# The mLSTM norm of a hybrid decoder layer in one piece of four chunks, with the last numerators between the two halves of the last output-gate product

## The reference, cut to what matters

```
h   = num / max(|den|, exp(-m))
mu  = mean(h);  var = mean((h - mu)^2)            # per token and head, 128 values
h   = (h - mu) * rsqrt(var + LN_EPS) * ml_norm_g
y_ml = sigmoid(o_m) * h                            # o_m: output-gate projection of the stream
q_lat = einsum('bthd,hdc->bthc', q_a, w_uk)        # queries of the attention, per head
s = einsum('bqhc,bqkc->bqhk', q_lat, kv_sel) * scale; p = softmax(s)
return concat([y_att, y_ml]) @ w_out
```

## Time and profile before

| what | value |
|---|---|
| median of 3 runs | 1124.44 us (1123.28 to 1125.76) |
| profiled execution, its own time | 1123.59 us |
| its span, first to last instruction | 1121.9 us |
| mean granted TensorE clock | 0.985 |
| TensorE busy | 1079.1 us (96%) |
| VectorE busy | 468.6 us (42%) |
| ScalarE busy | 347.4 us (31%) |
| GpSimd busy | 134.1 us (12%) |

### The profile page before, as it was taken

How to read it: one execution, slowest core, us unless ns; L and a number is a source line. 1 busy time by engine, 2 the same in 40 slices (tenths; PEclk the granted TensorE clock), 3 DMA queues, 4 the chain that set the end, 5 groups by cost and what they waited for, 6 DMA issues and landing times.

```text
span 1121.9 us, 15986 instructions
## 1 busy us (share of the span) xinstructions
PE 1079.1 (96%) x6569; PEld 931.7 (83%) x6569; DVE 468.6 (42%) x725; ACT 347.4 (31%) x453; POOL 134.1 (12%) x98
## 2 busy tenths in 40 slices
PE   8999999999999999999988999999999999999993
PEld 7999999999999987689865568768888888888882
DVE  3332332323232253699885533553333333322235
ACT  3222322222121234434337532452223232221211
POOL 4000000000011115212313004240000000000001
PEclk9999999999999999989998999999999999999997
DMA  6424233231322323122210101223333333143311
GB/s 191 113 75 111 76 87 100 75 100 52 104 79 86 106 75 97 38 79 73 76 38 1 38 1 46 67 75 89 99 92 95 96 91 100 59 134 89 92 51 75
DMA packets 159165, 90.34 MB, mean 81 GB/s; under 512 B 6596, under 2 KB 156792, under 8 KB 159128
## 3 DMA queue, kind: packets, MB, share of 16 engines
q1 hardware_dynamic: 159128, 89.83, 28.1%
HBM read 87.72 MB, written 2.10 MB: 80 GB/s over the span
## 4 chain that ended last, share of the span: by engine, by line
PE 88%; DVE 6%; ACT 3%; POOL 2%; issue 1%; DMA 0%; DVEq 0%; SPq 0%; POOLq 0%
PE ps L919 75%; PE ps L1054 4%; POOL xl L484 2%; PE ps L1328 2%; PE ps L1308 1%; PE ps L1319 1%; DVE x L1545 1%; DVE zrow L1503 1%; PE ps L1336 1%; DVE sil L1539 1%; PE ps L1116 1%; ACT whi L617 1%; DMA xin<-in_x 0%; DVE x L1528 0%; PE ps L1218 0%
## 5 line engine op out<-in xcount | busy, mean ns | idle before, releaser
L919 PE MATMUL ps<-xl,whi 128*128 128x264 f32 (+1 forms) x1264 | 350.9, 330 | 8.9 <-POOL xl L484 8.0
L919 PE MATMUL ps<-xh,whi 128*128 128x264 f32 (+1 forms) x1264 | 356.1, 331 | 2.7 <-DVE wlo L1412 1.6
L919 PE MATMUL ps<-xh,wlo 128*128 128x264 f32 (+1 forms) x1264 | 353.3, 329 | 0.0
L919 PEld LDWEIGHTS ps<-xl,whi 128*128 128x128 f32 x1264 | 212.4, 190 | 36.4 <-POOL xl L484 16.1
L919 PEld LDWEIGHTS ps<-xh,whi 128*128 128x128 f32 x1264 | 212.8, 189 | 30.0 <-issue 5.9
L919 PEld LDWEIGHTS ps<-xh,wlo 128*128 128x128 f32 x1264 | 213.8, 189 | 21.7 <-issue 0.2
L1403 DVE TENSOR_TENSOR wlo<-wraw,whi 128x2048 fp32r<-128x2048 f32 (+1 forms) x81 | 171.5, 2117 | 144.0 <-ACT whi L617 144.0
L617 ACT ACTIVATE whi<-wraw 128x2048 fp32r<-128x2048 f32 (+1 forms) x89 | 152.4, 1712 | 129.6 <-PE ps L919 123.8
L919 PE MATMUL ps<-hh,whi 128*128 128x264 f32 (+1 forms) x528 | 141.5, 322 | 0.0
L919 PE MATMUL ps<-hl,whi 128*128 128x264 f32 (+1 forms) x528 | 141.2, 321 | 0.0
L919 PE MATMUL ps<-hh,wlo 128*128 128x264 f32 (+1 forms) x528 | 140.4, 320 | 0.0
(11 more groups left out here) (217 smaller groups left out, 873.8 us busy)
## 6 DMA issues: line engine op xcount, KB each, us to landing
wraw<-in_ffn_w_gate SPq DMA_DIRECT2D x44, 512.0 KB, 4.0
wraw<-in_ffn_w_up SPq DMA_DIRECT2D x43, 512.0 KB, 5.2
wraw<-in_ffn_w_down SPq DMA_DIRECT2D x32, 384.0 KB, 3.4
wraw<-in_ffn_w_down SPq DMA_DIRECT2D x32, 320.0 KB, 3.8
wraw<-in_w_in SPq DMA_DIRECT2D x19, 512.0 KB, 4.7
wraw<-in_w_out SPq DMA_DIRECT2D x8, 512.0 KB, 4.0
xin<-in_x SPq DMA_DIRECT2D x2, 1024.0 KB, 6.1
out<-zrow SPq DMA_DIRECT2D x8, 256.0 KB, 2.0
```

The lines of the kernel that those rows point to most:

```text
L919: mm = pe.matmul(ps[:, b + e, 0:width], w, mov, start=(first and n == 0), stop=(last and n == 2))
```

## The change

The numerators of chunk 4 move from behind the whole product `o_half(19)` to between its fourth and fifth step. On ScalarE their copy `copy_num(4)` moves ahead of the sigmoid `o_out(19)`, and the square root, which was taken once before that sigmoid (three chunks) and once between the copies of the latent queries (the last chunk), is taken once behind the sigmoid, for all chunks. On VectorE the norm is one piece of four chunks; the operations that apply it are moved into the attention: heads 0 and 1 (eight operations) ahead of group 0, heads 2 and 3 (eight operations) behind the first two masked scores.

```
 # ScalarE
                 copy_num(3)
-                mlstm_sd(0, 3)
+                copy_num(4)
                 o_out(19)
-                copy_num(4)
+                mlstm_sd()
                 for h in range(ATT_H):
-                    if h == 4:
-                        mlstm_sd(3, 4)
                     act.wait_ge(ql_done, h + 1)
...
-            def mlstm_sd(j0, j1):
-                act.wait_ge(ml_var, 1 if j0 == 0 else 2)
-                v = mls[:, 0, :].rearrange("p (h j) -> p h j", h=ML_H)[:, :, j0:j1]
-                act.activation(v, v, ACT.Sqrt).then_inc(ml_sd, 1)
+            def mlstm_sd():
+                act.wait_ge(ml_var, 1)
+                act.activation(mls[:, 0, :], mls[:, 0, :], ACT.Sqrt).then_inc(ml_sd, 1)
 # TensorE
                 numerators(3)
-                o_half(19)
+                o_half(19, 0, 4)
                 numerators(4)
+                o_half(19, 4, KT)
                 lat_queries()
 # VectorE
-                mlstm_norm(0, 3)
-                normed_mlstm(range(ML_H), 0, 3)
-                mlstm_norm(3, 4)
+                mlstm_norm()
...
+            def mlstm_norm():
+                for j in range(4):
                     dve.wait_ge(num_copied, 2 * (j + 1))
                     for h in range(ML_H):
                         dve.bn_stats(bst[:, h * 4 + j, :], nums[:, h, j, 0:ML_DV]).then_inc(dv, 1)
...
+                for q in range(ML_H * 4):
+                    dve.bn_aggr(mv[:, q, :], bst[:, q, :]).then_inc(dv, 1)
...
+            def normed_mlstm(heads):
                 for h in heads:
-                    for j in range(j0, j1):
+                    for j in range(4):
                         q = h * 4 + j
                         v = nums[:, h, j, 0:ML_DV]
                         ins = dve.tensor_scalar(v, v, mv[:, q, 0:1], mls[:, 2, q:q + 1], ALU.subtract, ALU.mult)
-                    if j1 == 4:
-                        ins.then_inc(hn_ready, 1)
+                    ins.then_inc(hn_ready, 1)
 # VectorE, attention()
+                normed_mlstm((0, 1))
                 late = None
...
-                        if G == 0:
-                            normed_mlstm((2 * half, 2 * half + 1), 3, 4)
+                        if (G, half) == (0, 0):
+                            normed_mlstm((2, 3))
```

More of the change, by code:

```diff
@@ L1677, in mlstm @@
                     select(4, r0, r1)
-                mlstm_norm(0, 3)
-                normed_mlstm(range(ML_H), 0, 3)
-                mlstm_norm(3, 4)
-            def mlstm_norm(j0, j1):
-                for j in range(j0, j1):
+                mlstm_norm()
+            def mlstm_norm():
+                for j in range(4):
                     dve.wait_ge(num_copied, 2 * (j + 1))
@@ L1688, in mlstm_norm @@
                 dve.wait_ge(dv, n_dv[0])
[L1689 to L1692, removed]
+                for q in range(ML_H * 4):
+                    dve.bn_aggr(mv[:, q, :], bst[:, q, :]).then_inc(dv, 1)
+                    n_dv[0] += 1
                 dve.wait_ge(dv, n_dv[0])
-                hj = lambda v: v.rearrange("p (h j) -> p h j", h=ML_H)[:, :, j0:j1]
@@ L1695, in mlstm_norm @@
-                em = tok[:, :, :].rearrange("p j e -> p e j")[:, 4:8, 1 + j0:1 + j1]
-                den = nums[:, :, j0:j1, ML_DV]
+                hj = lambda v: v.rearrange("p (h j) -> p h j", h=ML_H)
+                em = tok[:, :, :].rearrange("p j e -> p e j")[:, 4:8, 1:NT]
+                den = nums[:, :, :, ML_DV]
                 link(dve.scalar_tensor_tensor(hj(mls[:, 0, :]), den, -1.0, den, ALU.mult, ALU.max))
                 link(dve.tensor_tensor(hj(mls[:, 0, :]), hj(mls[:, 0, :]), em, ALU.max))
-                link(dve.reciprocal(hj(mls[:, 1, :]), hj(mls[:, 0, :])))
@@ L1700, in mlstm_norm @@
[L1700 to L1705, removed]
@@ L1707, in normed_mlstm @@
-            def normed_mlstm(heads, j0, j1):
+                link(dve.reciprocal(mls[:, 1, :], mls[:, 0, :]))
+                link(dve.tensor_tensor(mls[:, 0, :], mls[:, 1, :], mls[:, 1, :], ALU.mult))
+                link(dve.tensor_tensor(mls[:, 0, :], mls[:, 0, :], mv[:, :, 1], ALU.mult))
+                dve.tensor_scalar(mls[:, 0, :], mls[:, 0, :], EPS, None, ALU.add).then_inc(ml_var, 1)
+                dve.wait_ge(ml_sd, 1)
+                link(dve.reciprocal(mls[:, 2, :], mls[:, 0, :]))
@@ L1708, in normed_mlstm @@
+                link(dve.tensor_tensor(mls[:, 2, :], mls[:, 2, :], mls[:, 1, :], ALU.mult))
+            def normed_mlstm(heads):
                 for h in heads:
-                    for j in range(j0, j1):
+                    for j in range(4):
                         q = h * 4 + j
```

## The result

| kernel | median us | runs |
|---|---|---|
| before | 1124.37 | 5 (1121.94 to 1125.76) |
| changed | 1116.19 | 5 (1113.73 to 1116.98) |

The ratio is 0.9932, with a 95% interval of 0.9916 to 0.9948: 5.9 to 9.4 us faster.

What follows compares the result with a forecast made beforehand. The prediction took ScalarE's order, ahead of copies TensorE waits for, to bound the stretch. Waits gave 6.5 us, the clock took back 1.0, so 5.5 us off 1124.44 made 1118.9 us, range 1117.0 to 1121.6.

Steps and rivals of the forecast that it cites:

- The waits, the term of 6.5 us: From the last gate product to the attention's fifth mask: removed waits let that mask start 6.5 us earlier.
- mask 5: VectorE's fifth mask in the attention: starts at 595.38 against 601.87, 6.5 us earlier.
- the copy of the numerators: ScalarE's copy of the last chunk's numerators, ahead of the sigmoid: runs from 581.57 to 582.24.
- the norm's readiness for its square root: VectorE's statistics and aggregations for all four chunks: ready for the square root at 585.75, with 0.7 us of cover.
- the square root behind its load: On ScalarE behind the sigmoid: table load from 585.15 to 586.43, then the square root at once, at 586.43.
- the second score: TensorE's second attention score, needing the seventh query copy: starts at 590.05 against 594.80, 4.75 us earlier.
- the eight operations between masks 2 and 3: VectorE's norm-applying operations behind the second mask, eight in place of two: 2.11 us, from 591.05 to 593.16.
- TensorE's wait for the first copy: At the latent queries: TensorE waits about 1 us (586.2 to 587.2), in place of the old waits.
- the gain ends at the second score: Rival, chance 0.10: VectorE's chain from there to the fifth mask keeps 7.07 us, leaving 3.75 us of gain: 1120.7 us.
- What the clock takes back, the term of 1.0 us: Behind the first weighing: half clock from 593.9 to 600.5 costs 1.0 us, with bounds of 0 and 3.3 us.
- The sum's base, 1124.44 us: Median time of the kernel before, from which the forecast gain of 5.5 us was subtracted.
- the hole as ScalarE's order: TensorE's 3.09 us hole at 584.15: blamed on two table switches and a square root waiting for VectorE, ahead of needed copies.

Runs made afterwards that it cites:

- the kernel in the old order: Changed kernel with numerators put back behind the whole gate product and their copy behind the sigmoid, norm still in one piece: 1120.49 us, 0.9975 of the kernel before.

## Why the prediction was wrong, by its own steps

**The waits, the term of 6.5 us: right, 6.67 measured at mask 5 and 6.69 at the weighing.** Every piece of it stands in the timelines within 0.2 us: the copy of the numerators, the norm's readiness for its square root, the square root behind its load, the second score, the eight operations between masks 2 and 3, mask 5 (21.63 us behind the scores; forecast 595.38 - 573.57 = 21.81). TensorE's wait for the first copy was put at 1 us and is 0.78. The rival "the gain ends at the second score" did not come: 1.9 us of the 6.7 arise behind it.

**What the clock takes back, the term of 1.0 us: near in size over the profiles (0.85), and that by luck; wrong in place and form.** The clock was to fall at 593.9, 20.3 us behind the scores, and be back at 600.5. In eight profiles it held 1.00 through the stretch up to 26.9 us behind the scores at least, and where it fell it was down 3.4 us and not 6.6 (the dip that the 6.60 us were read from itself lasts 6.8 us, to 603.87; its window was cut at 603.60). A dip that costs 1.7 us and comes in half of the profiles happens to take on average nearly what one was to take that costs 1.0 and comes every time. A distance copied from one dip of another kernel does not place the next one. For one execution the term is 0 or 1.7, in none of the eight 1.0; in the execution first measured it is 0.

**The sum's base, 1124.44 us: this failed most.** It was the median of three runs, and the range below it left 6.5 us for the gain and 0.9 for all else. Over all sessions 86 different times of the kernel before have a mean of 1122.5 (1119.1 to 1126.4), and 22 of the changed kernel 1115.6 (1113.7 to 1118.4). The base was 1.9 us too high, and the profiled execution it was tied to had two dips early on (16 to 20 and 498 to 505 us), and reaches the point where the change begins at the late end of a scatter of 3.3 us. From 1122.5 the same sum gives 1117.0. Against the 1116.19 first measured that is 0.8 us off, against the mean of all 1.4. The result's own median before, 1124.37, is drawn from five runs that include the same three, so the 8.2 us between the medians are too many by the same draw: 6.9 us between the means.

**What is open.** The two means differ by 6.9 us, with 0.7 to either side at 95%. The eight profiles give 5.8 us. About 1 us lies between them, and it is on the changed kernel's side: its eight profiled executions took 1116.6 us on average, its 18 others 1115.4, while the three of the kernel before took 1122.4, close to the 1122.5 of all its runs. It would fit if the others have the dip behind the weighing less often (three of the eight took 1118.2 us or more, none of the 18 more than 1117.2), but no run shows where their dips lie. Nor is anything to be seen outside the stretch: the part behind the projection lasts 508.3 us in the three profiles before and 508.1 to 509.5 us in the eight after.

**A cause the prediction did not separate.** It read the hole as ScalarE's order, which is right, but 2.9 of the 6.7 us are the half clock that comes with the holes. Filling the holes won that part with every wait left as it was; the changed kernel wins it too, and pays 1.7 us of it back in half of its profiles.

## What to carry to other kernels

Before summing a gain against a median of three runs, look at how far executions of the same program are apart at the first changed instruction; measure from there, and let the range hold the base's scatter as well as the terms'. When several waits in one stretch are chained over three engines, reordering one engine moves the hole to the next wait: the order alone gave nothing, the norm in one piece alone 3.3 us of distance, both 6.7. A hole of TensorE costs its length and then, at half clock, part of what comes behind it (here 1.15 us behind a hole of 3.1); filling it with matmuls whose result nobody reads tells the two apart.

## What the runs showed of the hardware that was not expected

- The same program reaches the same instruction at times 3.3 us apart (570.4 to 573.7 us in these profiles), with dips of the granted clock to 0.50 at differing places ahead of it (between 11 and 21, 430 and 438, and 496 and 506 us). A copy of the kernel before measured 1.0016 of itself, with an interval (1.0003 to 1.0030) that leaves out 1: a ratio that is 0.15% off 1 is no evidence of a change here.
- A table load held ScalarE for 1.28 us and no longer: the next instruction started 0.01 to 0.02 us behind it. A load whose function waits was run ahead of the wait, at 581.68 with its square root at 585.16 in the kernel in the old order.
- GpSimd took 0.80 us for a subtract-and-scale of 128x128 with two operands per partition, VectorE 0.27 us, and 0.29 us while GpSimd did the same.
